# Differential attention: half of the scores' second pass split over the two halves of the array's rows, with one buffer of turned blocks

## The chip, the cores and the metric

The kernel runs on one core of a Trainium2 chip. The metric is the device time of one execution in microseconds; the kernel before was timed in three runs. A core has a matrix engine (PE; its weight loads are listed as PEld), a vector engine (DVE), a scalar engine (ACT), GpSimd (POOL), and a queue on SyncE (SP) that here only issues DMAs. All engines run at once and are ordered by semaphores alone.

## The reference, cut to what matters

Two transformer-like layers and a pooling and feed-forward layer act on 1024 rows of width 1024. The first layer is the one that is touched. After a projection and a rotation, each of four heads has two query and two key halves of width 64, and values of width 128; 256 context rows stand ahead of the 1024 rows, so there are 1280 keys:

```python
s = jnp.einsum('bqhmd,bkhmd->bhmqk', qblk, k, preferred_element_type=jnp.float32) * ATTN_SCALE
p = jax.nn.softmax(s, axis=-1)
a = p[:, :, 0] - lam * p[:, :, 1]
return jnp.einsum('bhqk,bkhv->bqhv', a.astype(v.dtype), v)
```

So for each head `h`, each block `t` of 128 queries and each half `m`, a 128x1280 block of scores is needed; the two softmaxes are mixed with the weight `-lam`, and the mix is multiplied with the values.

## The kernel before, in words

All matrices are kept in fp32, and products of precision beyond the single pass format are made from a high part and a low part. In `even_projections`, the queries of one head and half are turned so that the 64 channels lie on partitions: `q_turned[:, m, :]` has the high part on partitions 0 to 63 and the low part on 64 to 127. `k_turned[:, m, 0, :]` holds the high part of the keys twice (on partitions 0 to 63 and again on 64 to 127), and `k_turned[:, m, 1, :]` their low part, twice too. One 128-row matmul against part 0 thus gives `q_hi k_hi + q_lo k_hi`, and one against part 1 gives `q_hi k_lo + q_lo k_lo`. A block of 1280 scores takes three banks of PSUM (512, 512 and 256 columns) and two parts for each, six matmuls (`scores`, L1195). The stationary operand is the block of queries, the keys are streamed.

The work goes tile by tile, a tile being one block of 128 queries of one head, in an order written out by hand, the same on every engine. For the tiles 2 to 7 of each head PE does one `tile_step`: `scores(t, 0)`; `turn(t-2, 1)`, four transposes of the mixed block; `scores(t, 1)`; `turn(t-2, 2)`, two transposes; `values(t-2, 0..2)`, ten products with the values, that are recorded as twenty matmuls (L1223); `turn(t-1, 0)`, the first four transposes of the next block (L1211). DVE does, for each tile, a reduction of each half for the peaks (`peaks`, L1497), the combination of the tile before (L1505, L1507, and the mix in two pieces of 512 and 768 columns at L1517), and the copy of the first four transposed blocks out of PSUM into `mixed_t` (`turn_out`, L1532). ACT does the exponentials (L859), the other copies into `mixed_t` (L867) and the scaling of the output (L876, L879). The turn of the blocks 4 to 7 on PE waits for DVE's copy of the blocks 0 to 3, since both use the bank `MIX_BANK`.

`mixed_t` has two buffers, one for each parity of `t`. Between two heads PE turns the next head's keys and queries (L470), ACT makes their high parts (L488, L493) and DVE their low parts (L497, L504); then come the tiles 0 and 1 of the next head. The last tile of the last head (`is_last`) goes through other banks of PSUM. SP's program in this stage ends with two loads of weights for the next product (L704), issued when the last channel product of the Fourier part is done. The next stage begins behind a barrier of all engines.

Of the kernel before, what the change touches and what calls it, by code (L numbers as in the profile page):

```python
# [16 lines left out]
F32 = mybir.dt.float32  # L17
F32R = mybir.dt.float32r
AX_X = mybir.AxisListType.X

P = 128
D = 1024
KT = D // P
SEQ = 1024
RT = SEQ // P
CTX = 256
CT = CTX // P
BANK = 512
EPS = 1e-6
HEADS = 4  # L30
DH = 64
# [25 lines left out]
def program(nc, a, out):  # L57
    ctx = ExitStack()
    with ctx:
        sems = {}  # L60

        def sem(name):
            if name not in sems:
                sems[name] = nc.alloc_semaphore(name)
            return sems[name]
# [7 lines left out]
        def sb(stack, name, shape, dt=F32):  # L73
            return stack.enter_context(nc.sbuf_tensor(name, shape, dt))
# [266 lines left out]
        with ExitStack() as st:  # L341
            y_f = sb(st, "y_f", [P, F_GROUPS, SEQ])
            k_turned = sb(st, "k_turned", [P, 2, 2, KEYS], F32R)
            q_turned = sb(st, "q_turned", [P, 2, SEQ], F32R)
            OUT_FIRST = 2
            with ExitStack() as first:
                k_first = sb(first, "k_first", [P, 2, KEYT, 2, DH])
                sb(first, "below_ft", [P, 2 * D + BANK])
                ft_hi, ft_lo = (sb(first, "ft_" + part, [P, RADIX, 2, P], F32R) for part in ("hi", "lo"))
                u_odd = [sb(first, "u_odd_" + part, [P, RT, P], F32R) for part in ("hi", "lo")]  # L350
            with ExitStack() as heads:
                prob = sb(heads, "prob", [P, 2, 2, KEYS])
                mixed = sb(heads, "mixed", [P, 2, KEYS])
                mixed_t = sb(heads, "mixed_t", [P, 2, KEYS])
                k_head = sb(heads, "k_head", [P, 2, KEYT, 2, DH])
                q_head = sb(heads, "q_head", [P, 2, RT, 2, DH])
                o_square = sb(heads, "o_square", [P, DV])
                o_stat = sb(heads, "o_stat", [P, HEADS, RT])
                neg_peak = sb(heads, "neg_peak", [P, RT, 2])
                total = sb(heads, "total", [P, RT, 2])  # L360
                inverse = sb(heads, "inverse", [P, RT, 2])
                weight = sb(heads, "weight", [P, RT])
                subln_gain = sb(heads, "subln_gain", [P, 1])
                exp_first = sb(heads, "exp_first", [P, 1])
            with ExitStack() as behind:
                sb(behind, "below_out", [P, 15 * D])
                out_first = [(sb(behind, f"out_hi{m}", [P, KT, P], F32R), sb(behind, f"out_lo{m}", [P, KT, P], F32R))
                             for m in range(OUT_FIRST)]
            out_raw = []
            with ExitStack() as behind:  # L370
                sb(behind, "below_raw", [P, 15 * D])
                for m in range(OUT_FIRST):
                    sb(behind, f"beside_raw{m}", [P, KT, P])
                    out_raw.append(sb(behind, f"out_raw{m}", [P, KT, P]))
# [137 lines left out]
        def place(h, t, m):  # L512

            return score[1] if t == 1 and isinstance(h, int) and h == 0 else score[m]
# [22 lines left out]
        def is_last(h, t):  # L537
            return t == L1 and isinstance(h, int)

        def out_of(h, t):  # L540
            return ps[:, LAST_OUT_BANK, 0:P] if is_last(h, t) else ps[:, OUT_BANK, (t % 2) * P:(t % 2 + 1) * P]

# [15 lines left out]
        def even_projections():  # L558
            with ExitStack() as st:
# [53 lines left out]
                with nc.Block(name="even_in") as block:  # L613
                    @block.sync
                    def _(sp):
# [86 lines left out]
                        sp.wait_ge(sem("y_f_done"), F_GROUPS)  # L702
                        for m in range(OUT_FIRST):
                            sp.dma_start(out_raw[m][:, :, :], w_out_even[:, :, m * P:(m + 1) * P]).then_inc(sem(f"out_landed{m}"), 16)  # L704

                    @block.scalar
                    def _(act):
# [154 lines left out]
                        def turn_out(h, t, i):  # L862

                            n = h * RT + t
                            b, e = rounds[i]
                            act.wait_ge(sem(f"mix_turned{i}"), n + 1 + (CREDIT if i == LAST else 0))
                            act.activation(mixed_t[:, t % 2, b * P:e * P],  # L867
                                           ps[:, i if is_last(h, t) else MIX_BANK, 0:(e - b) * P], ACT.Copy)\
                               .then_inc(sem(f"mix_copied{i}"), 1)

# [107 lines left out]
                    def _(pe):  # L978
# [204 lines left out]
                        def scores(h, t, m):  # L1183

                            n = h * RT + t
                            if t == 0:
                                pe.wait_ge(sem("q_low"), h * 2 + m + 1)
                            elif place(h, t, m) is score[m]:
                                pe.wait_ge(sem(f"exped{m}"), n)
                            else:  # L1190
                                pe.wait_ge(sem("exped1"), 2)
                            for b in range(0, KEYS, BANK):
                                e = min(b + BANK, KEYS)
                                for part in range(2):
                                    last = pe.matmul(place(h, t, m)[:, b:e], q_turned[:, m, t * P:(t + 1) * P],  # L1195
                                                     k_turned[:, m, part, b:e], start=(part == 0), stop=(part == 1))
                            last.then_inc(sem(f"scored{m}"), 1)

                        def turn(h, t, i):
# [15 lines left out]
                        def values(h, t, i):  # L1215

                            n = h * RT + t
                            pe.wait_ge(sem(f"mix_copied{i}"), n + 1 + (CREDIT if i == LAST else 0))
                            if i == 0 and not is_last(h, t):

                                pe.wait_ge(sem("o_scaled"), n + CREDIT)
                            for j in range(*rounds[i]):
                                last = pe.matmul(out_of(h, t),  # L1223
                                                 mixed_t[:, t % 2, j * P:(j + 1) * P], v_nat[:, j, bass.ds(h * DV, DV)],
                                                 start=(j == 0), stop=(j == KEYT - 1))
                            if i == LAST:
                                last.then_inc(sem("o_done"), 1)
# [70 lines left out]
                    def _(dve):  # L1298
# [226 lines left out]
                        def turn_out(h, t):  # L1525

                            n = h * RT + t
                            b, e = rounds[0]
                            dve.wait_ge(sem("mix_turned0"), n + 1)

                            dve.wait_ge(sem("o_done"), n - 1 + CREDIT)
                            dve.tensor_copy(mixed_t[:, t % 2, b * P:e * P], ps[:, 0 if is_last(h, t) else MIX_BANK, 0:(e - b) * P])\  # L1532
                               .then_inc(sem("mix_copied0"), 1)

                        def tile_step(h, t, h1, t1):
# [2165 lines left out]
```

## Time and profile before

| what | value |
|---|---|
| three timed runs | 1807.63, 1809.46, 1817.28 us, median 1809.46 |
| the profiled execution, first to last instruction (its span) | 1803.4 us |
| PE, PEld, DVE, ACT, POOL busy | 97%, 81%, 67%, 44%, 42% of the span |
| mean granted clock of PE | 0.991 of full speed |

The span is the profiled execution's own time, from the first to the last instruction; the timed runs' median is 6.1 us above it, for what lies around the span. The busy share of PE is not its share of peak speed, as matmuls overlap in a pipeline and their ends are modelled. The time from the start of one matmul to the start of the next is the better measure of what it costs. The attention part that is changed lies between about 369 and 582 us of the span.

### The profile page before, as it was taken

The numbers are of one execution on the slowest core, as the hardware profiler recorded it, in microseconds if no ns is written. First come the engines' busy times: TensorE is split into PE (matmuls) and PEld (weight loads), VectorE is DVE, ScalarE is ACT, GpSimd is POOL, SyncE is SP. The second block draws the span as 40 slices with busy tenths as digits, with TensorE's granted clock in tenths as the row PEclk, the third lists the DMA queues.
The fourth block names the chain that finished last, engine by engine and source line by source line (L and its number), as shares of the span: only waits on it lengthen the run. The fifth ranks groups of instructions, "written<-read, shape, count | busy, mean of one in ns | idle before, by whom it ended". The sixth has DMA issues, their size and how long they took to land.

```text
span 1803.4 us, 22828 instructions
## 1 busy us (share of the span) xinstructions
PE 1742.9 (97%) x8677; PEld 1461.8 (81%) x8677; DVE 1212.7 (67%) x1390; ACT 800.6 (44%) x1253; POOL 759.5 (42%) x450
## 2 busy tenths in 40 slices
PE   6999999989998899999999999999999999999999
PEld 4788887888888688788888889978888888878887
DVE  3734799578898616854545743786666667689865
ACT  3522222667677325533333432754435444444443
POOL 2332422000001142466666520548999999810000
PEclk8999999999999999999999999999999999999999
DMA  9567123000000731222221611303232232286433
GB/s 358 204 216 238 48 83 117 4 24 1 0 0 1 245 106 47 59 82 59 60 81 59 198 59 47 117 24 106 82 93 83 72 92 82 85 329 223 147 122 123
DMA packets 165385, 188.32 MB, mean 104 GB/s; under 512 B 9454, under 2 KB 117543, under 8 KB 165159
## 3 DMA queue, kind: packets, MB, share of 16 engines
q1 hardware_dynamic: 165287, 187.00, 31.7%
q8 instruction: 64, 1.05, 0.2%
q14 instruction: 34, 0.28, 0.1%
HBM read 152.37 MB, written 34.60 MB: 104 GB/s over the span
## 4 chain that ended last, share of the span: by engine, by line
PE 53%; DVE 4%; ACT 2%; issue 1%; DMA 1%; SPq 0%; ACTq 0%; DVEq 0%
PE ps L3217 20%; PE ps L2225 15%; PE ps L3268 10%; PE ps L2285 5%; PE ps L3568 1%; PE ps L3230 1%; DVE cv_lo_p L132 1%; DVE up_lo_p L132 1%; DVE residual L2147 0%; ACT residual L3404 0%; PE ps L3234 0%; DVE residual L3126 0%; DMA w_raw<-in_ffn_w_out 0%; ACT cv_hi_p L129 0%; ACT residual L1964 0%
## 5 line engine op out<-in xcount | busy, mean ns | idle before, releaser
L3217 PE MATMUL ps<-up_hi_p,st_hi_p 128*128 128x512 f32 x560 | 218.7, 391 | 2.9 <-ACT residual L2935 2.9
L3217 PE MATMUL ps<-up_lo_p,st_hi_p 128*128 128x512 f32 x560 | 218.5, 390 | 0.0
L3217 PE MATMUL ps<-up_hi_p,st_lo_p 128*128 128x512 f32 x560 | 218.3, 390 | 0.0
L3268 PE MATMUL ps<-down_ring 128*128 128x512 f32 x924 | 210.9, 390 | 2.8 <-DVE down_ring L132 2.6
L3268 PEld LDWEIGHTS ps<-down_ring 128*128 128x128 f32 x924 | 173.0, 188 | 40.5 <-issue 4.0
L132 POOL TENSOR_TENSOR in_lo<-in_raw,in_hi 128x512 fp32r<-128x512 f32 (+1 forms) x54 | 96.9, 1803 | 215.5 <-ACT in_hi L129 215.5
L2225 PE MATMUL ps<-cv_hi_p,cv_st_hi_p 128*128 128x512 f32 x392 | 153.2, 391 | 2.7 <-ACT residual L1943 2.7
L2225 PE MATMUL ps<-cv_hi_p,cv_st_lo_p 128*128 128x512 f32 x392 | 153.0, 390 | 0.0
L2225 PE MATMUL ps<-cv_lo_p,cv_st_hi_p 128*128 128x512 f32 x392 | 153.0, 390 | 0.0
L2067 DVE TENSOR_TENSOR residual<-ps,residual 128x512 f32<-128x512 f32 x70 | 48.3, 691 | 120.0 <-PE ps L2225 120.0
L132 POOL TENSOR_TENSOR st_lo_p<-up_raw,st_hi_p 128x512 fp32r<-128x512 f32 x68 | 101.7, 1499 | 64.4 <-ACT st_hi_p L129 64.4
L3217 PEld LDWEIGHTS ps<-up_hi_p,st_hi_p 128*128 128x128 f32 x560 | 105.5, 188 | 25.4 <-issue 3.3
L3217 PEld LDWEIGHTS ps<-up_lo_p,st_hi_p 128*128 128x128 f32 x560 | 105.6, 189 | 21.9
L3217 PEld LDWEIGHTS ps<-up_hi_p,st_lo_p 128*128 128x128 f32 x560 | 105.6, 189 | 21.9
L3068 DVE TENSOR_TENSOR residual<-ps,residual 128x512 f32<-128x512 f32 x100 | 68.4, 686 | 69.5 <-PE ps L3217 69.2
L1497 DVE TENSOR_REDUCE neg_peak<-ps 128x1 f32<-128x1280 f32 x64 | 95.2, 1487 | 9.8 <-PE ps L1195 8.6
L983 PE MATMUL ps<-in_hi,h_hi 128*128 128x512 f32 x256 | 99.8, 390 | 1.6 <-issue 0.9
L983 PE MATMUL ps<-in_hi,h_lo 128*128 128x512 f32 x256 | 99.6, 389 | 0.0
L983 PE MATMUL ps<-in_lo,h_hi 128*128 128x512 f32 x256 | 99.6, 389 | 0.0
L859 ACT ACTIVATE prob<-ps,neg_peak 128x1280 f32<-128x1280 f32 x64 | 84.9, 1326 | 29.5 <-DVE neg_peak L1497 29.2
L3087 DVE SCALAR_TENSOR_TENSOR residual<-residual,cols 128x1023 f32<-128x1023 f32 x44 | 72.5, 1648 | 35.8 <-ACT residual L2949 29.8
L132 POOL TENSOR_TENSOR cv_st_lo_p<-cv_raw,cv_st_hi_p 128x512 fp32r<-128x512 f32 x50 | 74.7, 1501 | 51.8 <-ACT cv_st_hi_p L129 51.7
(396 smaller groups left out, 4232.4 us busy)
## 6 DMA issues: line engine op xcount, KB each, us to landing
up_raw<-in_ffn_w_in SPq DMA_DIRECT2D x44, 512.0 KB, 5.0
w_raw<-in_ffn_w_out SPq DMA_DIRECT2D x66, 256.0 KB, 2.8
cv_raw<-in_odd_w_in SPq DMA_DIRECT2D x32, 512.0 KB, 5.5
in_raw<-in_even_w_in SPq DMA_DIRECT2D x48, 256.0 KB, 3.9
y_scratch<-residual SPq DMA_DIRECT2D x22, 512.0 KB, 2.6
ada_raw<-in_ada_w SPq DMA_DIRECT2D x16, 512.0 KB, 9.1
square<-in_ada_w SPq DMA_DIRECT2D x16, 512.0 KB, 4.3
rest_odd<-in_ada_w SPq DMA_DIRECT2D x16, 512.0 KB, 4.4
```

Source lines behind the costliest of these rows:

```text
L132: return eng.tensor_tensor(dst, src, high.bitcast(F32), ALU.subtract).then_inc(done, 1)
L859: act.activation(prob[:, t % 2, m, :], place(h, t, m), ACT.Exp, bias=neg_peak[:, t, m:m + 1], accum_out=total[:, t, m:m + 1]).then_inc(sem ...
L983: last = pe.matmul(ps[:, bank, :], x[:, k, r * P:(r + 1) * P], w[:, n % RING, :], start=(k == 0 and x is x_hi and w is in_hi), stop=(k == ...
L1497: dve.tensor_reduce(neg_peak[:, t, m:m + 1], place(h, t, m), AX_X, ALU.max, negate=True)\
L2067: dve.tensor_tensor(dst, ps[:, bank(g, p), :], base, ALU.add).then_inc(sem(name), 1)
L2225: last = pe.matmul(out, w[a_], x[b_], start=(first and a_ == 0 and b_ == 0), stop=(stop and a_ == 1), skip_group_check=skip)
L2285: last = pe.matmul(ps[:, 2 * (d % 4) + c, :], w[a_], x[k][:, c * BANK:(c + 1) * BANK], start=(k == 0 and a_ == 0 and x is y_hi), stop=(k = ...
L3068: dve.tensor_tensor(dst, ps[:, bank(j, p), :], base, ALU.add).then_inc(sem(name), 1)
L3087: dve.scalar_tensor_tensor(out=y[:, 1:SEQ], in0=x[:, 0:SEQ - 1], scalar=col(FFN_TAP1, first + j), in1=y[:, 1:SEQ], op0=ALU.mult, op1=ALU.a ...
L3217: last = pe.matmul(ps[:, bank(j, p), :], w[p][:, kk * P:(kk + 1) * P], x[p][:, kk, :], start=(first and w is st_hi and x is up_hi), stop=( ...
L3230: pe.matmul(ps[:, plain_bank(j, kind, side), :], part[FIRST_SLOT[j][kind, half]][:, ks], x_hi, start=(kk == 0 and half == 0 and part is st ...
L3268: last = pe.matmul(ps[:, 4 * (i % 2) + m, :], slot[:, s, m * P:(m + 1) * P], slot[:, x, :], start=(k == 0 and s == 0 and x == 2 and DOWN[i ...
```

## The change

For the tiles 2 to 7 of each head, the second pass (part 1) over the first two banks is made by two matmuls of 64 rows each. The first uses partitions 0 to 63 (`q_hi` with `k_lo`) for bank 0. The second uses partitions 64 to 127 for bank 1, with a copy of `q_hi` that a DMA has put on those partitions (`q_upper[m]`). The product of the two low parts is not made there any more. The third bank keeps its full second pass, and the tiles 0 and 1 keep six full matmuls. The loops over part and bank change places for all tiles. Each head gets two DMAs of 64 partitions x 4 KB, issued by SP behind the weight loads, and PE waits for each at tile 2. `mixed_t` becomes a single buffer, which makes room for `q_upper0`; the last tile of the last head writes its turned blocks into `prob`, and DVE's copy waits for one more tile's values to be done.

```diff
-                mixed_t = sb(heads, "mixed_t", [P, 2, KEYS])
+                mixed_t = sb(heads, "mixed_t", [P, KEYS])
+                q_upper0 = sb(heads, "q_upper0", [P, SEQ], F32R)
+                sb(heads, "beside_q_upper", [P, KEYS - SEQ])
...
+                q_upper1 = sb(behind, "q_upper1", [P, SEQ], F32R)
+            q_upper = [q_upper0, q_upper1]
...
+        def turned_mix(h, t):
+            return prob[:, L2 % 2, 0, :] if is_last(h, t) else mixed_t
...
+                        for h in range(HEADS):
+                            for m in range(2):
+                                if h == 0:
+                                    sp.wait_ge(sem("head_high"), m + 1)
+                                else:
+                                    sp.wait_ge(sem(f"scored{m}"), h * RT)
+                                    sp.wait_ge(sem("q_high"), (h - 1) * 2 + m + 1 + CREDIT)
+                                sp.dma_start(q_upper[m][DH:P, :].bitcast(F32), q_turned[0:DH, m, :].bitcast(F32)).then_inc(sem(f"q_raised{m}"), 16)
...
-                            for b in range(0, KEYS, BANK):
-                                e = min(b + BANK, KEYS)
-                                for part in range(2):
-                                    last = pe.matmul(place(h, t, m)[:, b:e], q_turned[:, m, t * P:(t + 1) * P],
-                                                     k_turned[:, m, part, b:e], start=(part == 0), stop=(part == 1))
+                            tiled = t >= 2
+                            if t == 2:
+                                pe.wait_ge(sem(f"q_raised{m}"), h * 16 + 16)
+                            rows = slice(t * P, (t + 1) * P)
+                            for part in range(2):
+                                for b in range(2 * BANK if tiled and part else 0, KEYS, BANK):
+                                    e = min(b + BANK, KEYS)
+                                    last = pe.matmul(place(h, t, m)[:, b:e], q_turned[:, m, rows], k_turned[:, m, part, b:e],
+                                                     start=(part == 0), stop=(part == 1))
+                            if tiled:
+                                pe.matmul(place(h, t, m)[:, 0:BANK], q_turned[0:DH, m, rows], k_turned[0:DH, m, 1, 0:BANK],
+                                          start=False, stop=True)
+                                last = pe.matmul(place(h, t, m)[:, BANK:2 * BANK], q_upper[m][DH:P, rows],
+                                                 k_turned[DH:P, m, 1, BANK:2 * BANK], start=False, stop=True)
                             last.then_inc(sem(f"scored{m}"), 1)
...
-                            dve.wait_ge(sem("o_done"), n - 1 + CREDIT)
-                            dve.tensor_copy(mixed_t[:, t % 2, b * P:e * P], ps[:, 0 if is_last(h, t) else MIX_BANK, 0:(e - b) * P])\
+                            dve.wait_ge(sem("o_done"), n + CREDIT - int(is_last(h, t)))
+                            dve.tensor_copy(turned_mix(h, t)[:, b * P:e * P], ps[:, 0 if is_last(h, t) else MIX_BANK, 0:(e - b) * P])\
```

ACT's copies (L867) and PE's products with the values (L1223) read and write `turned_mix(h, t)` in place of `mixed_t[:, t % 2]`.

## Rows read from the trace of the kernel before

**Rows 1.** Table by stretch, all engines: the attention part and what follows it.
```profile
core 0: us, PE busy (x) PEld busy (x) DVE busy (x) ACT busy (x) POOL busy (x), PEclk, DMA share, GB/s
360.00:582.00 222.00, 203.09 (x1447) 183.39 (x1445) 196.93 (x239) 155.86 (x299) 18.13 (x14) 0.99 0.02 5
```
**Rows 2.** Table by stretch, two tiles of head 1 in turn, columns as above.
```profile
443.98:449.63 5.65, 5.65 (x45) 5.30 (x44) 5.20 (x8) 4.06 (x10) 0.00 (x0) 1.00 0.00 0
449.63:455.54 5.91, 5.84 (x45) 5.32 (x44) 5.72 (x8) 4.57 (x10) 0.00 (x0) 1.00 0.00 0
```
**Rows 3.** PE in order of time, the same tiles: start us, duration us, count at the end.
```profile
443.98 1.41 PE L1195 MATMUL ps<-k_turned,q_turned 128*128 128x512 f32 x6
445.23 0.60 PE L1211 MATMUL ps<-ident,mixed 128*128 128x128 f32 x4
445.58 1.41 PE L1195 MATMUL ps<-k_turned,q_turned 128*128 128x512 f32 x6
446.83 0.38 PE L1211 MATMUL ps<-ident,mixed 128*128 128x128 f32 x2
447.05 2.40 PE L1223 MATMUL ps<-residual,mixed_t 128*128 x20
449.28 0.60 PE L1211 MATMUL ps<-ident,mixed 128*128 128x128 f32 x4
449.63 1.40 PE L1195 MATMUL ps<-k_turned,q_turned 128*128 128x512 f32 x6
451.11 0.63 PE L1211 MATMUL ps<-ident,mixed 128*128 128x128 f32 x4
...
455.54 1.41 PE L1195 MATMUL ps<-k_turned,q_turned 128*128 128x512 f32 x6
```
**Rows 4.** DVE in order of time from the same stretch, columns as above.
```profile
445.43 1.49 DVE L1497 TENSOR_REDUCE neg_peak<-ps 128x1 f32<-128x1280 f32 x1 [0.38 <-PE ps L1195]
...
450.28 0.68 DVE L1532 COPY mixed_t<-ps 128x512 f32<-128x512 f32 x1
...
451.08 1.49 DVE L1497 TENSOR_REDUCE neg_peak<-ps 128x1 f32<-128x1280 f32 x1
```
**Rows 5.** PE within one group of scores, three narrow windows of the timeline.
```profile
445.58 0.71 PE L1195 MATMUL ps<-k_turned,q_turned 128*128 128x512 f32 x2
...
445.90 0.62 PE L1195 MATMUL ps<-k_turned,q_turned 128*128 128x512 f32 x2
446.13 0.63 PE L1195 MATMUL ps<-k_turned,q_turned 128*128 128x512 f32 x2
446.36 0.51 PE L1195 MATMUL ps<-k_turned,q_turned 128*128 128x512 f32 x2
...
446.60 0.40 PE L1195 MATMUL ps<-k_turned,q_turned 128*128 128x256 f32 x2
```
**Rows 6.** PE in narrow windows around matmuls of 32 array columns, four side by side.
```profile
272.13 0.39 PE L116 MATMUL ps<-h_hi,in_lo 128*128 128x512 f32 x1
...
272.35 0.39 PE L116 MATMUL ps<-h_hi,in_lo 128*128 128x512 f32 x1
272.67 0.64 PE L1088 MATMUL ps<-rest_sum,ones 128*32 128x512 f32 x4
...
273.56 1.04 PE L1088 MATMUL ps<-rest_sum,ones 128*32 128x512 f32 x8
...
273.98 0.61 PE L1088 MATMUL ps<-rest_sum,ones 128*32 128x512 f32 x4
...
274.53 0.50 PE L116 MATMUL ps<-h_hi,in_hi 128*128 128x512 f32 x1
...
274.87 0.40 PE L116 MATMUL ps<-h_hi,in_hi 128*128 128x512 f32 x1
```
**Rows 7.** SP, then the table by stretch, at the beginning of attention.
```profile
369.72 1.00 SPq L704 DMA_DIRECT2D out_raw<-in_even_w_out  x2
...
371.15:373.00 1.85, 1.43 (x6) 1.05 (x6) 1.54 (x2) 0.65 (x1) 1.85 (x3) 1.00 1.03 303
373.00:374.50 1.50, 0.00 (x0) 0.00 (x0) 1.43 (x4) 1.50 (x3) 1.39 (x2) 1.00 1.04 279
374.50:376.90 2.40, 0.66 (x4) 0.42 (x4) 2.12 (x3) 2.35 (x3) 0.00 (x0) 0.94 0.04 10
376.90:379.20 2.30, 2.30 (x6) 1.91 (x7) 0.22 (x1) 0.00 (x0) 0.00 (x0) 0.50 0.00 0
```
**Rows 8.** Timeline of head 1: the last high part of its queries, its tile 2.
```profile
419.85 1.04 ACT L493 ACTIVATE q_turned<-ps 128x1024 fp32r<-128x1024 f32 x1
...
432.42 1.40 PE L1195 MATMUL ps<-k_turned,q_turned 128*128 128x512 f32 x6
```
**Rows 9.** Timeline of head 3, one of two tiles beside the split of the next weights.
```profile
567.44 0.63 PE L1211 MATMUL ps<-ident,mixed 128*128 128x128 f32 x4 [1.21 <-DVE mixed_t L1532]
...
569.05 2.74 DVE L1517 SCALAR_TENSOR_TENSOR mixed<-prob,weight 128x512 f32<-128x512 f32 x1
```

More of the change, by code:

```diff
@@ L866, in turn_out @@
                             act.wait_ge(sem(f"mix_turned{i}"), n + 1 + (CREDIT if i == LAST else 0))
-                            act.activation(mixed_t[:, t % 2, b * P:e * P],
+                            act.activation(turned_mix(h, t)[:, b * P:e * P],
                                            ps[:, i if is_last(h, t) else MIX_BANK, 0:(e - b) * P], ACT.Copy)\
@@ L1223, in values @@
                                 last = pe.matmul(out_of(h, t),
-                                                 mixed_t[:, t % 2, j * P:(j + 1) * P], v_nat[:, j, bass.ds(h * DV, DV)],
+                                                 turned_mix(h, t)[:, j * P:(j + 1) * P], v_nat[:, j, bass.ds(h * DV, DV)],
                                                  start=(j == 0), stop=(j == KEYT - 1))
```

## The prediction

> **What bounds the kernel now.** I read the table by stretch first, then PE and DVE in order of time inside one head, then the places where PE works in parts of the array. In the attention part PE is busy 203 of 222 us and DVE 197, and their clock is full but for one place [rows 1]. Shares that close together don't say which of the two sets the pace, so the tile is what has to be read. The tiles come in two lengths in turn, 5.65 and 5.91 us [rows 2], mean 5.78. In the short one PE has no gap: scores 1.25 us from start to start (443.98 to 445.23), four transposes 0.35, scores 1.25, two transposes 0.22, values 2.23, four transposes 0.35, together 5.65 [rows 3]. This sum is PE's floor. In the long one the first scores last 1.48 from start to start (449.63 to 451.11), 0.23 more, because the transposes behind them wait for DVE's copy: it begins at 450.28, takes 0.68 and ends at 450.96, and the transposes start 0.15 later [rows 3, 4].
>
> The wait comes back in every second tile by this loop. A tile's first scores start at 443.98; the reduction of them starts 1.45 later (445.43); from there DVE works without a gap to the end of the copy, 445.43 to 450.96, 5.53; 0.15 more and the transposes go, 7.13 after the scores of the tile before; from these transposes (451.11) to the next first scores (455.54) PE needs 4.43. Sum 11.56 for two tiles, and 443.98 to 455.54 is 11.56 [rows 3, 4]. So PE's floor is 5.65 a tile, DVE's loop 5.78, and DVE alone would allow about 5.55 (its chain of 5.53 and a step to the next reduction). PE and DVE are nearly in balance. That is the first result: a faster PE can win at most 5.78 - 5.55 = 0.23 us a tile, and a slower one costs nothing until its floor has risen by 0.13.
>
> As all engines meet at a barrier behind this stage, what a tile loses or wins goes straight into the time. 24 tiles of 32 are touched (2 to 7 of four heads), each with two groups of scores.
>
> **The change, part by part.**
>
> *What is removed.* Two of a group's matmuls of 512 columns start 0.23 apart (445.90, 446.13, 446.36), those of 256 columns take the rest of the group, 446.60 to 446.83, 0.23 for both [rows 3, 5]. The first one's start shows 0.32 to the next, as it holds a weight load. The change leaves two full 512s, both 256s and the pair: 1.25 - 2 x 0.23 = 0.79 for the four full ones, and then the pair in place of 0.46.
>
> *What is added.* If the pair runs side by side, it streams for 0.22 (one matmul of 512 and some ns until the second starts). But it needs the array divided, and no row of this kernel shows row halves. The nearest are the matmuls with 32 array columns, four side by side in four column groups [rows 6]. Three prices can be read there. On the way in, the last full matmul starts at 272.35 and the first of the divided ones at 272.67, 0.32 against the 0.22 between two full ones (272.13 to 272.35): about 0.09. On the way out, four start at 273.98 and the four before at 273.56, so a group needs 0.43 and would be through by 274.41, with the last of the four some 0.02 later; the next full one is recorded at 274.53: 0.10. And the weights of the first full one had not been loaded ahead: it takes 0.50 in place of 0.39, and the second one follows at 274.87, 0.34 later in place of 0.23: 0.11 for a load of 128 columns. The pair's own load is of 128 columns too, and I expect it behind the first drain, bare as well: 0.11 (both halves at once). In attention the load in front of the transposes is hidden today, since they follow the scores without a gap; behind a divided matmul it would be bare.
>
> Sum for a group: 0.09 + 0.11 + 0.22 + 0.10 + 0.11 = 0.63, in place of 0.46: 0.17 longer. The rows are rounded to 0.01, which leaves 0.15 to 0.17; I take 0.16. Bounds: with no drain and all loads hidden, 0.22 - 0.46 = -0.24. With the two halves one after the other behind a common load, 0.16 + 0.21 = +0.37; if the second's load is bare too, +0.48.
>
> A rule of the Trainium skill speaks against this change, and the trace agrees with it at the column groups [rows 6]: the Trainium skill, TensorEngine Tiling (Array Packing), Key Properties, says that a change of tiling mode, not of the tile alone, drains the engine. By it the sum stays as above; without it, it would be the lower bound. No run here yet shows it for row halves.
>
> *What that does to a tile.* PE's floor becomes 5.65 + 2 x 0.16 = 5.97. The scores themselves aren't ready later: today the last two end at 446.60 + 0.40 = 447.00, 1.42 into the group [rows 5]; then the pair starts to stream at 0.79 + 0.09 + 0.11 = 0.99 and needs 0.39 with its tail, end 1.38. So DVE's chain starts some 0.03 earlier, and its loop is (7.13 - 0.03 + 4.43 + 0.16)/2 = 5.87, below 5.97. PE then sets the pace with no wait for the copy. Short tiles lose 0.32, long ones 0.06. A head has three of each: 3 x 0.32 + 3 x 0.06 = 1.14, four heads 4.6. In head 3 two tiles have a wait of over 1.2 us in the first scores, as DVE's mix is drawn out to 2.74 us (one of the two is shown) [rows 9]; it swallows what PE adds there, 2 x 0.19 = 0.4 less. Remains +4.2.
>
> *The DMAs and the wait at tile 2.* In heads 1 to 3 a copy is issued when the queries' high part is made (419.85 + 1.04 for head 1's half 1), and tile 2 starts at 432.42, over 11 us later [rows 8]: nothing. In head 0, SP has the two weight loads in front, 1.00 for both issues from 369.72, so the copies are issued about 370.7 and 371.2. The DMA engines are full until about 374.5 at 280 to 300 GB/s; 0.5 MB more at that rate is 1.8 us, until 376.3. Tile 2 starts at 376.90, and half 1 is needed over 2 us later [rows 7]. Both are in time by the rate; bounds 0 and +1 (a copy from SBUF to SBUF is not in the trace). Behind the waiting matmul stand all of PE's work and then DVE's reduction; that stretch runs at half clock already (0.50), where the longer group costs perhaps 0.3 more. I take +0.3 for both together. SP has nothing else behind the copies in this stage.
>
> *One buffer of turned blocks.* DVE's copy now waits for the values of the tile just before. In PE's order `turn(t-1, 0)` stands behind `values(t-2)`, and the copy waits for that turn anyway: nothing added. ACT's copies are behind later turns, so the same holds. For the last tile of all, the target is `prob`'s half that the mix of tile 6 has already read, and its wait is the old one: nothing. If this cover were missing, the copy would wait for 2.4 us of values each tile, but the order of one engine can't be broken. The order of part and bank costs nothing in tiles 0 and 1, with the same six matmuls.
>
> The profiled execution has a span of 1803.4; the median of the timed runs is 1809.46, 6.1 above. Added to the median: 1809.5 + 4.2 + 0.3 = **1814.0**.
>
> **The rivals.**
>
> *A, the division is free.* No drain at the switch, loads ahead. A group shrinks by 0.24 to 1.01, PE's floor to 5.17. The scores are ready at 0.79 + 0.39 = 1.18 in place of 1.42, the loop is (7.13 - 0.23 + 4.43 - 0.24)/2 = 5.55, and DVE's own chain allows no less. -0.23 x 24 = -5.5: 1804.0. For it: nothing in rows but that four column groups do start within 0.02 of each other; against it, both edges of the divided stretch [rows 6]. The Trainium skill, TensorE: Matmul & The Clock Gate, Part 3, gives for a pack one matmul's duration and about 4 ns per tile; taken without the drain this is rival A's case.
>
> *B, the halves don't run side by side.* Both write all 128 partitions of PSUM, into two banks; the column groups of the trace write different partitions. If the second half streams behind the first, a group gains 0.37 to 0.48, the floor becomes 6.39 to 6.61, against 5.78 that is 0.61 to 0.83 over 22 tiles: +13.4 to +18.3, 1823 to 1828. This is also the case that the change doesn't do what it says. It decides at 0.26 a group: from there a tile is 6.17, 0.39 over today's, and the loss passes 9 us.
>
> *C, in between:* side by side, but the second load behind the first, 0.11 more: 0.27 a group, floor 6.19, +0.41 x 22 = +9: 1819.
>
> **How the numbers follow.** My forecast has 0.50, A 0.14, B 0.26, C 0.10. Half a percent is 9 us, about what a measurement can tell from no change. Faster by more than that is beyond what DVE allows: 0.03. Slower by more holds B, most of C and a tail of the forecast: 0.34. Within: 0.63. The range reaches from just under A to B's upper part: 1803 to 1827; the forecast's own is 1811 to 1817.
>
> **What would show it.** PE in order of time: right if a group of scores lasts 1.41 from start to start, with two 64-row matmuls starting within 0.02 of each other some 0.2 behind the last full one, and the tiles are even, near 5.97, with no wait of L1211's transposes for the copy. A gap-free 1.01 and tiles of 5.55 with DVE never idle would show A; two 64-row matmuls 0.2 or more apart would show B. The reduction must start no later in the group than 1.45. A wait of tile 2 in head 0 for a DMA over 1 us, or any in other heads, would prove the DMA part wrong; DVE's copy waiting for the values would disprove the buffer part. The forecast is wrong if row halves switch at another price than column groups.

## The result and the profile after

Nine timed runs of the changed kernel have a median of 1817.19 us (1811.37 to 1821.84), nine of the kernel before 1809.29 (1807.63 to 1817.28). The ratio is 1.0039 with a 95% interval of 1.0023 to 1.0055: 7.1 us slower, 4.2 to 10. The forecast was 1814.0 in a range of 1803 to 1827, with 0.63 on "within half a percent". It held.

The profiled execution has a span of 1815.8 us, and its own time is 1817.5, 1.7 above. The span of before was 1803.4, but the difference of 12.4 is not what the change costs. From the first group of scores to the first transpose of the attention's output the starts in the trace give 228.4 us before and 232.9 after, so 4.5 us lie in the attention part. The rest has the same instructions and stands 6.0 longer behind it and 1.9 ahead of it. A second profile of the kernel before (below) has 228.8 us of attention, and its unchanged rest is 6.4 us longer behind attention and 1.9 ahead of it. So that part is what executions differ by, and the attention part is what can be read.

The granted clock accounts for most of the unchanged part. In the twelve profiles of this case the work behind attention takes 1214.6 to 1215.8 us where PE stands at half clock for 20.5 us of it, and 1220.8 to 1221.7 where it does for 37.5 (the changed kernel's 1221.3 goes with 30.7); kernels without a division stand at both ends. The timed runs show the same: over 67 runs of the kernel before, one of 4525.73 us left aside, a mean granted clock lower by 0.001 goes with 1.4 us more (a straight line fitted to them). By this line, an estimate, the nine runs of the changed kernel are 3.2 us longer than the kernel before at the same clock, and 2.2 more goes with their lower clock (mean 0.9857 against 0.9873). What is left of the 7.1 is well inside its interval. Whether the division has a part in that lower clock is open.

Two tiles of head 1 after, as a table by stretch (columns as in [rows 1]), answer to [rows 2]:

```profile
443.33:449.20 5.87, 5.87 (x45) 4.95 (x44) 5.44 (x8) 4.30 (x10) 0.00 (x0) 1.00 0.00 0
449.20:455.08 5.88, 5.88 (x45) 4.96 (x44) 5.47 (x8) 4.33 (x10) 0.00 (x0) 1.00 0.00 0
```

The tiles are even now, with PE busy throughout and DVE idle for 0.4. PE in order of time, for the second of them, answers to [rows 3]:

```profile
449.20 0.94 PE L1214 MATMUL ps<-k_turned,q_turned 128*128 128x512 f32 x4
450.08 0.49 PE L1217 MATMUL ps<-k_turned,q_turned 64*128 64x512 f32 x1
450.08 0.49 PE L1219 MATMUL ps<-k_turned,q_upper 64*128 64x512 f32 x1
450.50 0.66 PE L1235 MATMUL ps<-ident,mixed 128*128 128x128 f32 x4
450.92 0.94 PE L1214 MATMUL ps<-k_turned,q_turned 128*128 128x512 f32 x4
451.78 0.50 PE L1217 MATMUL ps<-k_turned,q_turned 64*128 64x512 f32 x1
451.79 0.50 PE L1219 MATMUL ps<-k_turned,q_upper 64*128 64x512 f32 x1
452.22 0.44 PE L1235 MATMUL ps<-ident,mixed 128*128 128x128 f32 x2
452.49 2.40 PE L1247 MATMUL ps<-residual,mixed_t 128*128 x20
454.73 0.60 PE L1235 MATMUL ps<-ident,mixed 128*128 128x128 f32 x4
```

The two halves start together. The pair stands 0.88 behind the group's start, and the transposes 0.42 behind the pair, in place of two full matmuls at 0.23 each. A group takes 1.30 (449.20 to 450.50) in place of 1.25. The four transposes take 0.42 in place of 0.35, the two 0.27 (452.22 to 452.49) in place of 0.22. That is 0.11 for each divided group, twice a tile, and 5.65 + 0.22 = 5.87.

DVE, answering to [rows 4], from the tile before that one:

```profile
444.75 1.49 DVE L1521 TENSOR_REDUCE neg_peak<-ps 128x1 f32<-128x1280 f32 x1 [0.36 <-PE ps L1219]
...
449.60 0.68 DVE L1556 COPY mixed_t<-ps 128x512 f32<-128x512 f32 x1
450.62 1.49 DVE L1521 TENSOR_REDUCE neg_peak<-ps 128x1 f32<-128x1280 f32 x1 [0.34 <-PE ps L1219]
```

The reduction starts 1.42 after its group (443.33 to 444.75; 1.45 before). The copy ends at 450.28, the transposes that need it start at 450.50. PE no longer waits for DVE; DVE waits for PE.

The other part of the loss is where I had put almost nothing. SP in order of time, then the waits of PE after 376 us (us in total, times, longest), then the stretch of tile 2 of head 0, against [rows 7]:

```profile
371.63 1.00 SPq L711 DMA_DIRECT2D out_raw<-in_even_w_out  x2
372.68 1.90 SPq L719 DMA_DIRECT2D q_upper<-q_turned  x2
```
```profile
PE ps L1214 <- DMA q_upper<-q_turned: 1.8, 1, 1.8
```
```profile
380.08:388.42 8.34, 8.34 (x42) 6.63 (x43) 4.95 (x6) 2.98 (x5) 0.00 (x0) 0.66 0.00 0
```

The copies are issued more slowly than the weight loads (1.90 us for the two, against 1.00), the first lands 7.4 us after its issue, at 380.03, and PE stands for 1.8 us. Tile 2 takes 8.34 at a mean of 0.66 of the clock, 7.09 at 0.78 before. The clock did not fall in the 3.2 us in which PE waited for ACT; it was full until 377.6 and fell at 378.9, in the wait for the copy. The stretches, columns as in [rows 1]:

```profile
376.00:377.60 1.60, 0.00 (x0) 0.00 (x0) 1.53 (x5) 1.60 (x2) 0.29 (x1) 1.00 1.16 278
377.60:380.10 2.50, 0.68 (x5) 0.44 (x5) 1.15 (x2) 1.16 (x2) 0.00 (x0) 0.76 0.45 93
```

Before, it fell at 376.6, also ahead of tile 2 and without a wait for a DMA. What differs is how much of the half clock lies in tile 2: 5.7 us in the changed kernel, 3.1 before.

### The profile page after: what moved, and what is told of

Read it like the earlier page. It is cut to its first block, busy times and chain, and to the rows that moved or that the text cites. A ratio compares the mean times of both kernels' runs of the same rounds, so it can differ in the third digit from the quotient of the medians.

```text
span 1815.8 us, 22850 instructions
## 1 busy us (share of the span) xinstructions
PE 1752.3 (97%) x8677; PEld 1458.5 (80%) x8677; DVE 1212.8 (67%) x1390; ACT 800.6 (44%) x1253; POOL 757.3 (42%) x450
## 4 chain that ended last, share of the span: by engine, by line
PE 53%; DVE 4%; ACT 2%; issue 1%; DMA 1%; SPq 0%; ACTq 0%; DVEq 0%
PE ps L3241 20%; PE ps L2249 14%; PE ps L3292 10%; PE ps L2309 5%; PE ps L3592 1%; DMA y_a<-y_scratch 1%; PE ps L3254 1%; DVE up_lo_p L132 1%; DVE cv_lo_p L132 1%; DVE residual L2171 0%; PE ps L3258 0%; ACT residual L3428 0%; DVE residual L3150 0%; ACT cv_hi_p L129 0%; ACT residual L1988 0%
## 5 line engine op out<-in xcount | busy, mean ns | idle before, releaser
L1521 DVE TENSOR_REDUCE neg_peak<-ps 128x1 f32<-128x1280 f32 x64 | 95.1, 1486 | 13.3 <-PE ps L1219 11.5
```

What stands on the lines that cost most here:

```text
L1521: dve.tensor_reduce(neg_peak[:, t, m:m + 1], place(h, t, m), AX_X, ALU.max, negate=True)\
```

## The experiments

Attention is measured from the first group of scores to the first transpose of the output, tile lengths from head 1, both in the one profiled execution.

| kernel | ratio to before (95%) | attention us | tile us |
|---|---|---|---|
| before, two profiles | 1 | 228.4, 228.8 | 5.65 and 5.91 |
| changed | 1.0039 (1.0023 to 1.0055) | 232.9 | 5.87 |
| copies first | 1.0023 (1.0007 to 1.0038) | 232.1 | 5.87 |
| six full matmuls, rest as changed | 0.9999 (0.9986 to 1.0013) | 229.9 | 5.66 and 5.90 |
| both halves on rows 0 to 63 | 1.0071 (1.0056 to 1.0087) | 244.0 | 6.34 |
| no copies, no wait | 1.0020 (1.0009 to 1.0030) | 231.2 | 5.88 |
| order of PE alone | 1.0045 (1.0031 to 1.0059) | 236.5 | 6.09 |
| one switch a tile | 1.0043 (1.0027 to 1.0058) | 237.0 | 6.06 |
| pair in the middle | one run | 234.0 | 5.99 |
| only half 0 divided | 1.0006 (0.9990 to 1.0022) | 228.5 | 5.77 |
| only half 1 divided | 1.0000 (0.9984 to 1.0017) | 230.4 | 5.76 and 5.92 |

**Copies of head 0 first.** The edit to the changed kernel:

```diff
+                        for m in range(2):
+                            sp.wait_ge(sem("head_high"), m + 1)
+                            sp.dma_start(q_upper[m][DH:P, :]...).then_inc(sem(f"q_raised{m}"), 16)
                         for m in range(OUT_FIRST):
                             sp.dma_start(out_raw[m][:, :, :], ...)
-                        for h in range(HEADS):
+                        for h in range(1, HEADS):
```

> The changed kernel, with head 0's two copies of the high queries issued ahead of the two weight loads in place of behind them. Theory S (the late copy in head 0 is a cost of its own, beside the switching of the array): the 1.8 us wait of PE at tile 2 of head 0 goes, the first scores of that tile start within 0.2 us of the time at which the kernel before has them (7.4 us after the first scores of tile 1 there), PE's clock is back at full speed about 3.4 us earlier, and the span is 2 to 3 us shorter than the changed kernel's, so 2 to 3 us above the kernel before. Rival W (the wait was covered by the clock or by the exponentials anyway): under 0.5 us off the changed kernel's time. Tiles stay at 5.87 us under both.

The wait went: tile 2 starts 7.52 us after the first scores of tile 1 there, 8.71 in the changed kernel and 7.44 before. With an empty queue the copies land 3.6 to 4.0 us after their issue. But the clock didn't come back earlier, it came back later in the tile, and tile 2 took 8.81 at 0.62 of the clock:

```profile
378.71:387.52 8.81, 8.81 (x42) 7.10 (x43) 5.08 (x7) 3.33 (x5) 0.00 (x0) 0.62 0.03 7
```

There 6.6 us of the tile are at half clock, 5.7 with the wait. So attention shrank by 0.7 in this profile and not by 2 to 3. The timed ratios, 1.0023 against 1.0039, have intervals that overlap; their difference of 2.9 us is the size expected but not shown. The wait was real; what it costs depends on how the clock falls.

**Six full matmuls.** Everything of the change but the division:

```diff
                             if tiled:
-                                pe.matmul(place(h, t, m)[:, 0:BANK], q_turned[0:DH, m, rows], ...)
-                                last = pe.matmul(place(h, t, m)[:, BANK:2 * BANK], q_upper[m][DH:P, rows], ...)
+                                for b in range(0, 2 * BANK, BANK):
+                                    last = pe.matmul(place(h, t, m)[:, b:b + BANK], q_turned[:, m, rows],
+                                                     k_turned[:, m, 1, b:b + BANK], start=False, stop=True)
```

> The changed kernel with all six matmuls of a group over 128 rows again (also tiles 2 to 7); the copies, the wait of PE at tile 2, the single buffer of turned blocks and the new order of part and bank stay. Theory S (the division of the array costs 0.11 us a group, the rest of the attention part's loss is the late copy): a group of scores takes 1.25 us again, tiles alternate 5.65 and 5.91, the wait in head 0 stays at about 1.8 us; the time is 2 to 2.5 us above the kernel before and 2 us under the changed one. Rival O (the new order, the single buffer or the copies' traffic slow the tiles): tiles stay over 5.8 in the mean and the time stays within 0.7 us of the changed kernel's.

PE in order of time, head 1:

```profile
442.33 0.94 PE L1214 MATMUL ps<-k_turned,q_turned 128*128 128x512 f32 x4
443.12 0.63 PE L1218 MATMUL ps<-k_turned,q_turned 128*128 128x512 f32 x2
443.80 0.63 PE L1234 MATMUL ps<-ident,mixed 128*128 128x128 f32 x4
444.18 0.94 PE L1214 MATMUL ps<-k_turned,q_turned 128*128 128x512 f32 x4
...
445.42 0.38 PE L1234 MATMUL ps<-ident,mixed 128*128 128x128 f32 x2
```

The group is 1.24 again (444.18 to 445.42), the one ahead of it has the old wait for the copy in it (1.47), and the tiles alternate as before. The wait for the DMA stays, 1.2 us once. Tile 2 of head 0 behind that wait is as long as in the second profile of the kernel before, which waits for no DMA (7.47, below):

```profile
380.81:388.23 7.42, 7.42 (x43) 6.66 (x43) 4.81 (x6) 2.99 (x5) 0.00 (x0) 0.75 0.00 0
```

So starting late adds nothing inside the tile by itself. The single buffer of turned blocks, the order of part and bank and the copies' traffic cost the tiles nothing, and by its ratio this kernel is that of before within 2.5 us. The division is what the time went into: attention is 3.0 us shorter than in the changed kernel, 0.9 of it in tile 2 of head 0. I had expected 2 to 2.5 us above before for the late copy; attention shows 1.1 to 1.5.

**Both halves on rows 0 to 63.** No copies, no wait; same products but in the same half of the array:

```diff
-                                last = pe.matmul(place(h, t, m)[:, BANK:2 * BANK], q_upper[m][DH:P, rows],
-                                                 k_turned[DH:P, m, 1, BANK:2 * BANK], start=False, stop=True)
+                                last = pe.matmul(place(h, t, m)[:, BANK:2 * BANK], q_turned[0:DH, m, rows],
+                                                 k_turned[0:DH, m, 1, BANK:2 * BANK], start=False, stop=True)
```

> The changed kernel with both 64-row matmuls on rows 0 to 63, so that they can only follow one another; no copies, no wait. Theory S (the halves do run side by side in the changed kernel, and this is what wins back 0.21 to 0.32 us of the switching's price): the second starts 0.2 to 0.33 us behind the first, a group takes 1.51 to 1.62 us in place of 1.30, a tile 6.3 to 6.5; with 22 to 24 tiles the attention part is 12 to 16 us longer than before's, less nothing for the copies: 1821 to 1825 us. Rival N (records of the changed kernel only show the same start, the array works them off one after the other): group and tile as in the changed kernel, 1.30 and 5.87.

```profile
448.85 0.94 PE L1204 MATMUL ps<-k_turned,q_turned 128*128 128x512 f32 x4
449.72 0.50 PE L1207 MATMUL ps<-k_turned,q_turned 64*128 64x512 f32 x1
450.05 0.39 PE L1209 MATMUL ps<-k_turned,q_turned 64*128 64x512 f32 x1
450.38 0.66 PE L1225 MATMUL ps<-ident,mixed 128*128 128x128 f32 x4
```

The second starts 0.33 behind the first, which holds 0.11 of bare load (0.50 long against 0.39), and the group is 1.53. That is 0.23 more than with two halves, the length of one matmul. So in the changed kernel they do run side by side: rival B falls. A tile is 6.34, as expected, and the time 13 us above before's. This also shows that the switch has its price without any second half.

**No copies.** The edit is the division as changed, with `q_turned[DH:P, m, rows]` for `q_upper[m][DH:P, rows]`, and neither copies nor the wait. The second bank then gets the product with the low part of the queries in place of the high one, so the sums are not the ones wanted, but the work of PE is the same.

> The changed kernel without copies and without the wait for them: the matmul on rows 64 to 127 takes what lies there, the low part of the queries, in place of the high part, so this product of the second bank is not the one wanted. Theory S: groups of 1.30, tiles of 5.87 as in the changed kernel, no wait at tile 2 of head 0; the attention part is 2 to 2.6 us longer than before's, and the time agrees with that of the kernel with the copies first within 0.7 us. Rival D (the copies' traffic in heads 1 to 3 costs too): it is over 1 us faster than the kernel with the copies first.

Tiles of 5.88, no wait, attention 231.2, 0.9 us under the kernel with the copies first. Heads 1 to 3 are the same to 0.1 us in both (from the first scores of head 1 to the output 169.0 in each); the 0.9 lie in head 0's tile 2, 7.87 here at a mean clock of 0.72, so with less time at half clock. The traffic of the copies costs nothing (rival D falls), and this is the division's cost by itself: 2.4 to 2.8 us of attention, 1.9 of them outside that tile, and 1.0020 by the ratio.

**The kernel before again.** No edit; one run.

> The kernel before, for a second profile. Theory H (how long PE stays at half clock at the beginning of attention, 3.4 us in the first profile of before and 6.8 in those of the changed kernel, is chance and belongs to neither): a second profile of before may show 6.8 as well, and then tile 2 of head 0 takes 7.4 us or more in place of 7.1. Rival K (the wait for the copies or the division prolongs it): 3.4 us again, 7.1 us for the tile. Tiles elsewhere 5.65 and 5.91 under both.

```profile
378.78:386.25 7.47, 7.47 (x42) 6.84 (x43) 5.54 (x7) 2.98 (x5) 0.00 (x0) 0.74 0.00 0
```

Tile 2 took 7.47 at a clock of 0.74, with no copy and no division; the first profile has 7.09 at 0.78. So a part of the spread belongs to neither kernel, as theory H has it. Tile 2 of the changed kernel took 0.9 more still, and not because divided groups are dear at half clock. Its first group there, against this one:

```profile
378.78 2.50 PE L1195 MATMUL ps<-k_turned,q_turned 128*128 128x512 f32 x6
381.08 1.05 PE L1211 MATMUL ps<-ident,mixed 128*128 128x128 f32 x4
381.79 1.82 PE L1195 MATMUL ps<-k_turned,q_turned 128*128 128x512 f32 x6
```
```profile
380.08 1.65 PE L1214 MATMUL ps<-k_turned,q_turned 128*128 128x512 f32 x4 [1.78 <-DMA q_upper<-q_turned]
...
382.38 1.12 PE L1235 MATMUL ps<-ident,mixed 128*128 128x128 f32 x4
383.15 1.63 PE L1214 MATMUL ps<-k_turned,q_turned 128*128 128x512 f32 x4
```

At half clock a group takes 2.30 undivided (378.78 to 381.08) and 2.30 divided (380.08 to 382.38); with the transposes it is 3.01 and 3.07. The 0.9 is the clock: 3.9 us of this tile are at half clock and 5.7 of the changed kernel's, and half of the 1.7 more, what full clock would have saved, is 0.9. Whether the division or the wait has a part in where the half clock ends isn't shown.

**Pair in the middle.** One run. With the copies first, the pair stands behind the two high matmuls of 512 and ahead of the two of 256.

> The changed kernel, copies of head 0 first, with the pair of 64-row matmuls in the middle of its group: behind the two high matmuls of 512 columns and ahead of the two of 256. Theory S (the price out of the divided stretch is a drain of 0.10 and the bare load of what follows, 0.06 for a transpose, 0.11 for a full matmul of the single pass format): pair to next full one 0.43 us, that one to its next 0.22 to 0.23 in place of 0.12; the group 1.35 to start of the transposes, these without a bare load of their own (0.35 for four), so that the tile stays within 0.05 us of 5.87. Rival T (the extra cost comes from the change to the transposes' format, not from the division): the group shrinks to 1.2 and the tile to under 5.7.

```profile
450.16 0.71 PE L1219 MATMUL ps<-k_turned,q_turned 128*128 128x512 f32 x2
450.80 0.49 PE L1221 MATMUL ps<-k_turned,q_turned 64*128 64x512 f32 x1
450.81 0.50 PE L1223 MATMUL ps<-k_turned,q_upper 64*128 64x512 f32 x1
451.24 0.51 PE L1226 MATMUL ps<-k_turned,q_turned 128*128 128x256 f32 x2
451.58 0.60 PE L1242 MATMUL ps<-ident,mixed 128*128 128x128 f32 x4
451.94 0.70 PE L1219 MATMUL ps<-k_turned,q_turned 128*128 128x512 f32 x2
```

The parts came out as priced: 0.43 from the pair to the next, 0.22 from the first 256 to the second (recorded in one row, 0.51 long with 0.28 for the last), the group 1.42, the transposes 0.36. Their sum is a tile of 5.99, not 5.87 within 0.05; I had added 1.35 where the rows give 1.42. Rival T falls, since the price is there without transposes behind the pair. So the format of what follows matters: a full matmul of the single pass format has 0.11 of load bare, a transpose only 0.06. Behind the group, where the change puts it, is the cheaper place.

**Order of PE alone**, on the kernel before and in the tiles 2 to 7 alone, and **one switch a tile**, which is that order on the changed kernel with the copies first. In the second edit `full` stands for the four undivided matmuls of a group and `halves` for the pair:

```diff
                             scores(h, t, 0)
-                            turn(h2, t2, 1)
                             scores(h, t, 1)
+                            turn(h2, t2, 1)
+                            values(h2, t2, 0)
                             turn(h2, t2, 2)
-                            for i in range(3):
+                            for i in (1, 2):
```
```diff
+                            elif m == 0:
+                                full(True, True)
+                                last = halves(False)
+                            else:
+                                halves(True)
+                                last = full(False, True)
```

> The kernel before with PE's order changed in the tiles 2 to 7, nothing divided: both groups of scores first, then the four transposes, the products with the blocks 0 to 3, the two transposes, the other products. Theory L (the kernel before is held at 5.78 us a tile by the loop over DVE's copy of the turned blocks, PE's own floor is 5.65): the transposes come 1.25 us later in the tile, so the wait for the copy goes, and all tiles are 5.65 to 5.67; 22 tiles x 0.12 = 2.7 us less than before. Rival X (the second group of scores then waits for the exponentials of the tile before, which now have 1.6 us less): tiles of over 5.8 us with waits in front of the second scores, time above before's.

> The same order of PE with the division of the changed kernel, and one switch of the array a tile: group 0 ends with its divided pair, group 1 begins with its own, so that the two pairs stand side by side; the copies of head 0 go ahead of the weight loads. Theory S (a switch in and out costs 0.33 us, drains and bare loads, and a pair itself 0.22 in place of 0.46): PE needs 5.35 to 5.45 us a tile, the pairs start 0.22 to 0.33 apart, and the tile is set by the exponentials that free the scores of the half 1, about 5.62; with head 0's slow tile as in the changed kernel that is 2 to 3.5 us less than before in all. Rival P (each pair is drained by itself, whatever stands beside it): pairs 0.42 apart, PE's floor over 5.6, tile 5.7 to 5.85, no gain over the kernel with the order alone.

Both lost, 1.0045 and 1.0043, and both for a wait that I had not looked for. ACT in the kernel with the order alone:

```profile
455.41 0.60 ACT L867 ACTIVATE mixed_t<-ps 128x512 f32<-128x512 f32 x1 [1.35 <-PE ps L1211]
456.54 0.38 ACT L867 ACTIVATE mixed_t<-ps 128x256 f32<-128x256 f32 x1 [0.53 <-PE ps L1211]
456.82 1.32 ACT L859 ACTIVATE prob<-ps,neg_peak 128x1280 f32<-128x1280 f32 x1
```

ACT's copies of the turned blocks stand in its program ahead of the exponentials that free the bank of the next tile's first scores. With the transposes later, the copies are later, the first exponential starts at 456.82 and ends at 458.14, and PE's next scores, which overwrite that bank, start at 458.28. The tile is 6.09. Theory L is missed by this wait, and rival X had it in front of the second scores, where it stands in front of the first, but X's cause was right: the exponentials come later.

One place in the kernel with one switch is free of that wait, the first divided tile of the heads 1 to 3 (head 0 has it at half clock). PE in order of time:

```profile
437.89 0.94 PE L1215 MATMUL ps<-k_turned,q_turned 128*128 128x512 f32 x4
438.76 0.50 PE L1220 MATMUL ps<-k_turned,q_turned 64*128 64x512 f32 x1
438.76 0.50 PE L1222 MATMUL ps<-k_turned,q_upper 64*128 64x512 f32 x1
439.10 0.39 PE L1220 MATMUL ps<-k_turned,q_turned 64*128 64x512 f32 x1
439.10 0.39 PE L1222 MATMUL ps<-k_turned,q_upper 64*128 64x512 f32 x1
439.42 0.97 PE L1215 MATMUL ps<-k_turned,q_turned 128*128 128x512 f32 x4
440.23 0.60 PE L1247 MATMUL ps<-ident,mixed 128*128 128x128 f32 x4
```

The second pair follows the first by 0.34, of which 0.11 is the first's bare load (0.50 against 0.39): 0.23 for a pair beside a pair, and the load of its weights is hidden. Both groups together take 2.34 (437.89 to 440.23). So the price is one of the switch, not of each pair (rival P falls), and one switch for two pairs is under two undivided groups, 2.50. In the later tiles the first scores and the second pair wait for exponentials.

**Only one half divided.** The condition `tiled = t >= 2` becomes `t >= 2 and m == 0`, or `m == 1`; with the copies first, for that half alone.

> The changed kernel with the division in half 0's scores only; half 1 has six full matmuls; copies for half 0 only, head 0's ahead of the weight loads. Theory L (two limits: PE's floor, 5.65 undivided and 0.11 more for each divided group, and the loop over DVE's copy, (7.12 + 4.43)/2 = 5.78 undivided): the floor is 5.76; in the loop the divided group 0 lies beside DVE's work and its scores are ready 0.03 earlier, so (7.09 + 4.43)/2 = 5.76; tiles are even at 5.76 to 5.78, and each switch of the tile costs nothing against before's mean of 5.78. Rival F (each divided group costs its 0.11 whatever the loop): mean of the tiles 5.89.

> The same with the division in half 1's scores only. Theory L: PE's floor is 5.76 as well, but the longer group now lies inside the loop, between the transposes that wait for DVE's copy and the next first scores, 4.43 + 0.11: (7.12 + 4.54)/2 = 5.83 to 5.84 in the mean, in turn about 5.76 and 5.9. So it is 0.06 us a tile, 1.4 us in all, above the kernel with only half 0 divided. Rival F: 5.89 as there, no difference between the two.

Two tiles of head 1 of each, by stretch, half 0 divided and then half 1:

```profile
445.69:451.46 5.77, 5.77 (x45) 5.13 (x44) 5.47 (x8) 4.34 (x10) 0.00 (x0) 1.00 0.00 0
451.46:457.23 5.77, 5.77 (x45) 5.13 (x44) 5.45 (x8) 4.31 (x10) 0.00 (x0) 1.00 0.00 0
```
```profile
446.77:452.54 5.77, 5.77 (x46) 5.09 (x44) 5.31 (x8) 4.17 (x10) 0.00 (x0) 1.00 0.00 0
452.54:458.45 5.91, 5.91 (x46) 5.09 (x44) 5.59 (x8) 4.44 (x10) 0.00 (x0) 1.00 0.00 0
```

Both to 0.01 as theory L has them: even tiles of 5.77, and a mean of 5.84 in turn. The same 0.11 us of PE is free in one place and costs half its size in the other, because only the second lies in the loop over DVE's copy. (Attention differs by 1.9 us between the two profiles, 0.6 of it in head 0's tile 2 with its clock.) In time the two can't be told from each other or from before (1.0006 and 1.0000).

No version here beats the kernel before: with half 0 alone the division costs nothing and gives nothing.

## Why the prediction was right, and where by luck

*The bound.* The loop of 11.56 us over two tiles and PE's floor of 5.65 were read rightly; the two kernels with one half divided show it best. A slower PE was free up to 0.12 a tile (5.77 against a mean of 5.78), I had said 0.13.

*The switch.* The terms ahead of the pair and inside it were right: pair at 0.88 (0.79 + 0.09), from there 0.42 to 0.43 to the next (0.11 + 0.22 + 0.10). That edges read at four column groups [rows 6] hold for two row groups was the gamble of the forecast, and it held. The rule that the prediction quotes from the Trainium skill, TensorEngine Tiling (Array Packing), Key Properties, is that a change of mode drains the engine. The trace agrees: at each of the 46 switches at full clock the pair starts 0.21 behind the last matmul of 256 columns, where two of those are 0.12 apart, and the same 0.21 is there with both halves on one side. The step that was mis-sized is the last term, "0.11 for a load of 128 columns" in front of the transposes: a transpose behind the pair shows its second 0.17 behind the first in place of 0.11, so 0.06. A group costs 0.11 and not 0.16, a tile 5.87 and not 5.97.

*The sum over the tiles.* From the first scores of head 1 to those of head 3, attention is 109.8 us long in place of 108.7, 0.55 a head; head 3 loses 0.25, as the drawn-out stretch there swallows a part, as forecast (its first long tile is 7.43 in both kernels). With 0.6 of head 0 behind its tile 2 that is 1.9 us, against the 4.2 of the forecast. The step that was too dear is the last term of a group: 0.05 less in each of 48 groups is the difference.

*The DMAs.* "Both are in time by the rate", with "+0.3 for both together", was wrong: tile 2 starts 1.3 us later, a wait of 1.8 where over 1 was to prove this part wrong. The bytes moved about as the rate said: the engines were full until 378.5, and the forecast's 376.3, set later by the 1.9 us by which this execution runs behind, is 378.2. What the sum left out is the time from there to the landing, at 380.03. The kernel before shows it too: its second weight load landed at 375.88, when the engines had been full until about 374.5. A copy has such a time of its own, 2.8 to 3.2 us from issue to landing in heads 1 to 3, where nothing else moves, and 3.6 to 4.0 ahead of the weights. Inside tile 2 there is 1.3 us more (0.9 against the second profile of before), and that is time at half clock, not the 0.3 for longer groups: those cost 0.06 each there.

So attention is 4.5 us longer where 4.5 was forecast (4.2 + 0.3), but as 1.9 for the division, 1.3 for the wait and 1.3 for the clock in one tile: two errors of opposite sign, and a match by luck. The timed difference of 7.1 us has 4.2 as its lower end. At the same granted clock it is 3.2 by the fitted line, as much as the 1.9 and the 1.3 together; most of the rest goes with the clock, and no run here shows what of that, if anything, belongs to the change. The 6.1 us that I put around the span is also such a difference: it is 1.7 in the same execution, and the profiled one of before was a quick one.

*The buffer.* The longer wait of DVE's copy never showed, as forecast; six full matmuls with the single buffer have the tiles of before. *The rivals:* A (free) falls by the 0.88 and the 0.42; B by the common start and by the kernel with one side; C, a second load behind the first, by 0.42 in place of 0.53.

## What to carry to other kernels

Halving the array's rows for a pair of matmuls saves one matmul (0.23 us at 512 columns) and costs a switch in and out (0.09 + 0.11 + 0.10 and a bare load of the next, 0.06 to 0.11). A single pair lost 0.11 a group here; two pairs side by side won PE 0.16 where nothing made it wait (2.34 in place of 2.50), though no kernel got faster by it. Before an engine is relieved, work out the loop that waits for it: here PE's tenth of a microsecond was free in half 0's scores, cost half in half 1's, and by DVE's own chain nothing that PE saves beyond 5.55 a tile could be had (the prediction's estimate; no kernel came near it). When an order is moved, follow every engine whose instructions wait for the moved ones, not the one that was the bound: ACT's two copies ate the reordering. And a small DMA's deadline is set by the time from issue to landing, which the kernel before already shows, and not by its rate alone.

## What the hardware showed that I had not expected

- The two 64-row matmuls start 0.003 us apart and end together. Their loads run together too; the pair behind a pair has its load hidden.
- The exit is cheaper into a transpose (0.06 of bare load) than into a full matmul (0.11).
- At half clock a divided group costs nothing against an undivided one (2.30 each), and 0.06 with the transposes behind it; at full clock it is 0.11.
- A DMA from SBUF to SBUF of 64 x 4 KB takes 2.8 to 3.2 us on idle queues, and SP needs 0.5 to 1.3 us to issue one.
- At the same place, after the same 3.2 us without work, PE's mean clock over tile 2 was 0.78 and 0.74 in two profiles of one kernel, and 0.51 to 0.78 in the other kernels. With both halves on one side it stood at 0.51 for the whole of an 11.5 us tile. Whether divided matmuls keep the clock down longer or chance does wasn't tried.
